# Gate broadcasts: four diagonals from VectorE and one 512-column product, in place of four 128-column products

## The chip, the cores and the metric

The kernel runs on one core of one Trainium2 chip. The metric is the device time of one execution in microseconds (us), from three timed runs of the kernel before: median 1494.13 us, 1493.53 to 1494.31 us. Lower is better. The engines are named as the profile names them: PE is TensorE (PEld its weight loads), DVE is VectorE, ACT is ScalarE, POOL is GpSimd, SP is SyncE, which issues most of the DMAs.

## The reference

The model is a two-layer trunk on 256 latent and 256 context tokens of width 1024, followed by one layer of a second model. The change touches only the modulation of the trunk. Per layer, six vectors of 1024 come from the condition; two of them, `ga1` and `ga2`, gate the two residual branches:

```python
mod = [m[:, None, :] for m in jnp.split(jax.nn.silu(c) @ w_mod[i] + b_mod[i], N_MOD, axis=-1)]
mod_c = jnp.split(jax.nn.silu(c_ctx) @ w_mod[i] + b_mod[i], N_MOD, axis=-1)
sh1, sc1, ga1, sh2, sc2, ga2 = mod
...
x = x + ga1 * rmsnorm(y, p["g_post_mix"])
xc = xc + ga1c * rmsnorm(yc, p["g_post_mix"])
...
x = x + ga2 * rmsnorm(sq_relu_mlp(hm, p["w_mlp1"], p["w_mlp2"]), p["g_post_mlp"])
```

All inputs are float32. In the last layer only the latent tokens go on, so that layer needs no context gates.

## The kernel before

**Layout.** Tokens lie on the 128 partitions in the residual stream (`X`, `Y`), so a gate, which differs by feature and not by token, must stand in the same row on all partitions: `GA` is [128, 4, 1024]; its four rows are the gates of sections 2 and 5 (`ga1`, `ga2`), each for latent and context. The modulation itself is computed by feature: `mod` has feature 128*kt + p on partition p, in one column per kt and per condition.

**Turning a gate.** One gate step makes half a gate, 512 features: column kt of `mod`, repeated over 128 columns, is the stationary operand, and the identity matrix `C_IDENT` the moving one. The product has in each row the 128 features of that column. Four such float32 products fill one bank of PSUM (L789), and ACT copies the bank to `GA` (L1316). PE waits for `mod_vec`, the semaphore of the finished column vectors.

**Where the gate steps run.** While the heads' attention runs, PE, ACT and DVE go through a list of small steps, `MOD_STEPS`, written out by hand in `fill_table`. The steps "rows" (32 weight loads against `cond`, reading two 1 MB chunks of the weight stream, L750), "features" (4 transposes, L756, then a reduction on DVE, L1991), "gate", and "cf_*" (parts of the conformer branch) all use bank 3 of PSUM. So they are a chain: PE starts step n only when ACT or DVE has read step n-1 (`mod_read`). Attention unit i has three slots for steps. In unit i PE runs scores (L945, L950), slot 0, transposes (L962), slot 1, values (L978), slot 2. DVE runs the maxima of the scores (L2139, L2140), slot 0, the probabilities (L2147, L2150), its half of the transposed probabilities (L2204), slot 1, outputs (L2210), slot 2. ACT runs slot 0, exponentials (L1522), L1585, slot 1, outputs (L1592), slot 2. Each engine runs its own list in order. In layer 0, gate steps stand in units 3, 4, 6, 7, 11, 12 (two) and 13; this text numbers them gate 1 to gate 8. Layer 1 has four: gates 9 and 10 inside the output projection (`OUT_STEPS`, L596), gates 11 and 12 at the first chunk of the MLP (`LAST_GATES`, called in `last_tile`).

**Weights.** SP loads the stream in chunks of 1 MB into four slots (L447), each when PE is through with the chunk that held the slot. ACT rounds a chunk to `w_hi` (L425), DVE subtracts to get `w_lo` (L435), and large products run in three passes of these pairs (L550, L570, L596).

**Names of DVE lines used below.** L1966 and L1967 are the statistics of the conformer's normalisation, L1981 the lower part of its last product, L1995, L1999 and L2003 finish a modulation vector. The order of all work is fixed in the program text; there is no scheduler.

Of the kernel before, what the change touches and what calls it, by code (L numbers as in the profile page):

```python
# [101 lines left out]
            MOD_STEPS += _steps  # L102
OUT_STEPS = range(len(MOD_STEPS), len(MOD_STEPS) + 3)
MOD_STEPS += [("features", DEPTH - 1, 5, 1), ("gate", DEPTH - 1, 2, 0), ("gate", DEPTH - 1, 2, 1)]
LAST_GATES = range(len(MOD_STEPS), len(MOD_STEPS) + 2)
MOD_STEPS += [("gate", DEPTH - 1, 5, half) for half in range(2)]

# [11 lines left out]
def mod_biased_count(n):  # L119

    return sum(kind == "features" and part == 1 for kind, l, sec, part in MOD_STEPS[START_STEPS:n])


def mod_vec_of(l, sec):
    return mod_vec_count(MOD_STEPS.index(("features", l, sec, 1)) + 1)
# [613 lines left out]
def pe_mod_step(k, pe, n, bank):  # L739

    kind, l, sec, part = MOD_STEPS[n]
    if n:
        pe.wait_ge(k.s("mod_read"), n)
    if kind == "rows":
        for j in range(2):
            c = At(mod_chunk(l, sec, part) + j)
            pe.wait_ge(k.w_loaded[c.slot], 16 * (c.first // SLOTS + 2))
            for kt in range(KT):
                g = kt % 4
                last = pe.matmul(k.banks(bank, 256, j * 256, slice(32 * g, 32 * g + 32)), k.cond[:, kt * 32:kt * 32 + 32],  # L750
                                 k.w[:, c.slot, kt * 256:kt * 256 + 256], start=kt < 4, stop=kt >= 4)
            last.then_inc(k.chunk_mm, 1)
    elif kind == "features":
        for kt in range(4):
            at = part * 512 + kt * 128
            last = pe.transpose(k.banks(bank, 128, kt * 128), k.rows[:, at:at + 128], k.C[:, C_IDENT:C_IDENT + 128])  # L756
        last.then_inc(k.s("mod_mm"), 1)
    elif kind == "cf_t":
        nq = 256 * CF_HALVES[l]
        k.wait(pe, "cf_conv", l, 1)  # L760
        for t in range(2):
            for kt in range(2):
                at = kt * nq + (2 * part + t) * 128
                last = pe.transpose(k.banks(bank, 128, t * 256 + kt * 128), mixer_buffers(k)["cf_acc"][:, at:at + 128],
                                    k.C[:, C_IDENT:C_IDENT + 128])
        last.then_inc(k.s("mod_mm"), 1)
    elif kind == "cf_b":
        k.wait(pe, "cf_norm", l, 1)
        for t in range(2):
            for kt in range(2):  # L770
                at = (2 * part + t) * 256 + kt * 128
                last = pe.transpose(k.banks(bank, 128, kt * 256 + t * 128), k.cft[:, at:at + 128],
                                    k.C[:, C_IDENT:C_IDENT + 128])
        last.then_inc(k.s("mod_mm"), 1)
    elif kind == "cf_pw":
        nq = 256 * CF_HALVES[l]
        k.wait(pe, "cf_act", l, CF_HALVES[l])
        for j in [part] if l == 0 else range(2):
            for kt in range(2):
                at = 1280 + kt * 256 + j * 128  # L780
                last = pe.matmul(k.banks(bank, nq, 0 if l == 0 else j * nq), k.SW[:, at:at + 128],
                                 mixer_buffers(k)["cf_acc"][:, kt * nq:kt * nq + nq], start=kt == 0, stop=kt == 1)
        last.then_inc(k.s("mod_mm"), 1)
    else:
        v, half = part // 2, part % 2
        pe.wait_ge(k.s("mod_vec"), mod_vec_of(l, sec))
        for kt in range(4):
            at = feature(l, sec) + (4 * half + kt) * 2 + v
            last = pe.matmul(k.banks(bank, 128, kt * 128), k.mod[:, at:at + 1].broadcast_to([128, 128]),  # L789
                             k.C[:, C_IDENT:C_IDENT + 128], start=True, stop=True)  # L790
        last.then_inc(k.s("mod_mm"), 1)


def start_rows(k, pe, n, j, bank):
# [488 lines left out]
def act_mod_step(k, act, n, bank):  # L1283
# [22 lines left out]
    elif kind == "cf_pw":  # L1306
        nq = 256 * CF_HALVES[l]
        act.wait_ge(k.s("mod_mm"), mod_mm_count(n + 1))
        hk = k.h_hi[:, :].rearrange("p (k n) -> p k n", k=KT)
        to = hk[:, 4 + part, :] if l == 0 else hk[:, 4:6, 0:nq]  # L1310
        src = k.banks(bank, 512) if l == 0 else k.banks(bank, 512).rearrange("p (k n) -> p k n", k=2)
        act.activation(to, src, ACT.Copy, scale=0.5).then_inc(k.s("cf_hi"), 1)
    elif kind == "gate":
        v, half = part // 2, part % 2
        act.wait_ge(k.s("mod_mm"), mod_mm_count(n + 1))
        act.activation(k.GA[:, 2 * GATE_SECTIONS.index(sec) + v, half * 512:half * 512 + 512], k.banks(bank, 512),  # L1316
                       ACT.Copy).then_inc(k.s("mod_read"), 1)


def act_start(k, act, o):  # L1320
# [632 lines left out]
    last.then_inc(k.s("cf_norm"), 1)  # L1953


def dve_mod_step(k, dve, n, bank, o=None):

    if n - 1 in [cf_statistics_at(layer) for layer in range(DEPTH)]:
        dve_cf_norm(k, dve, o, n >= FILL[1][0][0][0])
# [79 lines left out]
def dve_mixers(k, dve, o, l):  # L2039
# [206 lines left out]
        feed_lo(k, dve, out + 1, (1,))  # L2246
    dve_feed_rest(k, dve, out)
    transposed(end - 1)
    outputs(end - 1)


# [529 lines left out]
```

## Time and profile before

| what | value |
|---|---|
| timed runs | median 1494.13 us (1493.53 to 1494.31, 3 runs) |
| profiled execution | 1492.4 us, its span 1490.4 us |
| PE busy | 1434.9 us, 96% of the span |
| DVE busy | 908.4 us, 61% |
| ACT busy | 679.5 us, 46% |
| POOL busy | 37.1 us, 2% |
| granted TensorE clock, mean | 0.998 |
| the chain that ended last | PE 86%, ACT 5%, DVE 4%, DMA 3% |

The span runs from the first to the last instruction; the profiled execution's own time is 2.0 us more. "Busy" sums an engine's instructions with their modelled ends, so a busy PE may still be held back by others. In the chain of the work that ended last, each piece of time is put down to what released the next one. A row of the timeline gives start, duration, engine, line, operation, output and inputs, and in brackets how long the engine had been idle and what released it. The gate steps stand between 189.8 and 260 us (layer 0) and between 808 and 840 us (layer 1).

### The profile page before, as it was taken

What the parts mean: (1) busy time and instruction counts of PE and PEld (TensorE: products, weight loads), DVE (VectorE), ACT (ScalarE), POOL (GpSimd) and SP (SyncE); (2) the same over time, 40 slices, a digit from 0 to 9 for tenths busy, and PEclk for the clock granted to TensorE, in tenths of its full rate; (3) what the DMA queues carried; (4) which work ended last, traced back from release to release, by engine and by line L of the source; (5) the groups of instructions that cost most, each with busy time, mean ns of one, the idle gap of its engine ahead of it and who ended that gap; (6) DMA issues with size and microseconds to landing.
All of it is one profiled execution on the core that took longest, in us unless ns stands there. A gap on an engine that the chain in (4) does not pass through costs nothing.

```text
span 1490.4 us, 23388 instructions
## 1 busy us (share of the span) xinstructions
PE 1434.9 (96%) x9380; PEld 1229.4 (82%) x9380; DVE 908.4 (61%) x1394; ACT 679.5 (46%) x1084; POOL 37.1 (2%) x53
## 2 busy tenths in 40 slices
PE   5999998999999999999999999998999999999998
PEld 2787655888888888888866888997999999798996
DVE  2677455564232433468756665568998545796867
ACT  4421355553130322456145844456444564764544
POOL 0000000000000000000060000000000000000000
PEclk9999999999999999999999999999999999999999
DMA  9321575032331313236365555464445434455553
GB/s 394 144 87 71 213 296 227 1 142 85 113 97 43 142 56 141 85 113 220 123 245 237 198 187 180 147 221 170 170 170 171 146 138 142 142 197 190 178 198 114
DMA packets 33274, 235.91 MB, mean 158 GB/s; under 512 B 3680, under 2 KB 3680, under 8 KB 5408
## 3 DMA queue, kind: packets, MB, share of 16 engines
q1 hardware_dynamic: 32080, 228.31, 42.4%
q0 software_dynamic: 1104, 6.29, 1.3%
q8 instruction: 69, 1.13, 0.3%
q14 instruction: 21, 0.17, 0.0%
HBM read 233.54 MB, written 1.05 MB: 157 GB/s over the span
## 4 chain that ended last, share of the span: by engine, by line
PE 86%; ACT 5%; DVE 4%; DMA 3%; issue 1%; SPq 0%; DVEq 0%; ACTq 0%
PE ps L550 44%; PE ps L596 23%; PE ps L570 4%; DMA w<-in_stream 3%; PE ps L750 2%; PE ps L830 1%; PE ps L652 1%; PE ps L945 1%; PE ps L978 1%; ACT w_hi L425 1%; PE ps L962 1%; DMA w<-in_start 1%; PE ps L950 1%; PE ps L687 1%; PE ps L624 1%
## 5 line engine op out<-in xcount | busy, mean ns | idle before, releaser
L550 PE MATMUL ps<-h_hi,w_hi 128*128 128x256 f32 (+1 forms) x1504 | 468.6, 312 | 3.4 <-DVE h_lo L2436 0.9
L550 PE MATMUL ps<-h_hi,w_lo 128*128 128x256 f32 (+1 forms) x1504 | 464.7, 309 | 0.0
L550 PE MATMUL ps<-h_lo,w_hi 128*128 128x256 f32 (+1 forms) x1504 | 464.6, 309 | 0.0
L425 ACT ACTIVATE w_hi<-w 128x1024 fp32r<-128x1024 f32 x332 | 333.6, 1054 | 244.1 <-DMA w<-in_stream 244.0
L435 DVE TENSOR_TENSOR w_lo<-w,w_hi 128x1024 fp32r<-128x1024 f32 x332 | 391.0, 1221 | 87.7 <-ACT w_hi L425 83.3
L550 PEld LDWEIGHTS ps<-h_hi,w_hi 128*128 128x128 f32 x1504 | 287.0, 191 | 20.4 <-issue 2.9
L550 PEld LDWEIGHTS ps<-h_lo,w_hi 128*128 128x128 f32 x1504 | 287.0, 191 | 14.9 <-issue 0.5
L550 PEld LDWEIGHTS ps<-h_hi,w_lo 128*128 128x128 f32 x1504 | 286.9, 191 | 14.5
L596 PE MATMUL ps<-w_hi,g_hi 128*128 128x512 f32 x472 | 185.1, 392 | 1.8 <-DVE g_lo L2289 0.9
L596 PE MATMUL ps<-w_lo,g_hi 128*128 128x512 f32 x472 | 183.8, 389 | 0.0
L596 PE MATMUL ps<-w_hi,g_lo 128*128 128x512 f32 x472 | 183.8, 389 | 0.0
L596 PEld LDWEIGHTS ps<-w_hi,g_hi 128*128 128x128 f32 x472 | 88.6, 188 | 23.5 <-issue 3.2
L596 PEld LDWEIGHTS ps<-w_hi,g_lo 128*128 128x128 f32 x472 | 88.6, 188 | 18.7
L596 PEld LDWEIGHTS ps<-w_lo,g_hi 128*128 128x128 f32 x472 | 88.6, 188 | 17.7
L2288 DVE CAST g_hi<-R 128x1024 fp32r<-128x1024 f32 (+1 forms) x32 | 17.9, 561 | 127.0 <-ACT R L1659 127.0
L2267 DVE TENSOR_TENSOR Y<-ps,Y 128x512 f32<-128x512 f32 (+1 forms) x32 | 28.5, 889 | 99.0 <-PE ps L596 99.0
L1656 ACT ACTIVATE R<-ps 128x1024 f32<-128x1024 f32 (+1 forms) x32 | 26.0, 812 | 135.2 <-PE ps L550 126.0
L2069 DVE SCALAR_TENSOR_TENSOR U<-U,F 128x512 f32<-128x512 f32 (+1 forms) x120 | 65.0, 615 | 0.0
L570 PE MATMUL ps<-w_hi,h_hi 128*128 128x256 f32 x176 | 50.5, 287 | 0.0
L570 PE MATMUL ps<-w_lo,h_hi 128*128 128x256 f32 x176 | 49.8, 283 | 0.0
L570 PE MATMUL ps<-w_hi,h_lo 128*128 128x256 f32 x176 | 49.8, 283 | 0.0
L2463 DVE SCALAR_TENSOR_TENSOR R<-ps,F,R 128x254 f32<-128x254 f32 (+1 forms) x88 | 37.1, 477 | 14.1 <-ACT R L1797 13.4
(281 smaller groups left out, 1749.4 us busy)
## 6 DMA issues: line engine op xcount, KB each, us to landing
w<-in_stream SPq DMA_DIRECT2D x206, 1024.0 KB, 5.0
U<-in_start SPq DMA_DIRECT2D x4, 1024.0 KB, 11.7
w<-in_start SPq DMA_DIRECT2D x2, 1024.0 KB, 10.7
GA<-in_start SPq DMA_DIRECT2D x2, 1024.0 KB, 14.0
U<-in_bias POOLq DMA_DIRECT2D x2, 1024.0 KB, 6.2
SW<-in_small POOLq DMA_DIRECT2D x2, 896.0 KB, 4.9
X<-in_x SPq DMA_DIRECT2D x1, 1024.0 KB, 4.9
X<-in_ctx SPq DMA_DIRECT2D x1, 1024.0 KB, 7.1
```

Source lines behind the costliest of these rows:

```text
L425: act.activation(k.w_hi[:, c.slot, half], k.w[:, c.slot, half], ACT.Copy).then_inc(k.hi_done, 1)
L435: dve.tensor_tensor(k.w_lo[:, c.slot, half], k.w[:, c.slot, half], k.w_hi[:, c.slot, half].bitcast(f32), ALU.subtract).then_inc(k.lo_done, 1)
L550: last = pe.matmul(k.banks(2 * c.pair, n, j * (512 if tiles == 2 else n)), w[a][:, c.slot, at:at + 128], h[b][:, kt * stride:kt * stride + n],
L570: last = pe.matmul(k.banks(2 * c.pair, 256, t * (512 if n_tiles == 2 else 256)), h[a][:, at:at + 128], w[b][:, c.slot, kt * 256:kt * 256 + ...
L596: last = pe.matmul(unit_banks(k, c, tiles, t, half), h[a][:, at:at + 128], w[b][:, chunk.slot, local * 512:local * 512 + 512], start=kt == ...
L624: last = pe.matmul(unit_banks(k, c, 2, t, half), h[a][:, at:at + 128], w[b][:, chunk.slot, local * 512:local * 512 + 512], start=kt == 0 a ...
L750: last = pe.matmul(k.banks(bank, 256, j * 256, slice(32 * g, 32 * g + 32)), k.cond[:, kt * 32:kt * 32 + 32], k.w[:, c.slot, kt * 256:kt * ...
L1656: act.activation(k.R[:, j % 2, 0:2 * n].rearrange("p (t n) -> p t n", t=2), k.two(c, n), ACT.Relu).then_inc(k.act_read, 1)
L2069: ins = dve.scalar_tensor_tensor(acc[:, kt], src, w, acc[:, kt], ALU.mult, ALU.add)
L2267: dve.tensor_tensor(y, products, y, ALU.add).then_inc(k.dve_read, 1)
L2288: o.link(dve.tensor_copy(k.g_hi[:, cols:cols + 2 * n], r))
L2463: return dve.scalar_tensor_tensor(r, k.banks(2 * c.pair, 254 + tap, t * 512), k.F[:, bass.ds(tile, 1)], r, ALU.mult, ALU.add)
```

## The change

VectorE writes, into the very half row of `GA` that the gate will fill, the four 128x128 diagonal matrices that hold the gate's features: the identity, repeated four times, times the four columns, each repeated 128 times. It is one float32 operation on 128x512 elements. TensorE then multiplies once: a 128x128 matrix of ones, stationary, by these 512 columns. Each column has one element that is not zero, so the product has the gate in every row. ACT copies the bank to the same half row of `GA` as before. PE now waits for `diag`, a count of diagonals; the wait for `mod_vec` moves to VectorE. ACT's program is the same.

```diff
 OUT_STEPS = range(len(MOD_STEPS), len(MOD_STEPS) + 3)
 MOD_STEPS += [("features", DEPTH - 1, 5, 1), ("gate", DEPTH - 1, 2, 0), ("gate", DEPTH - 1, 2, 1)]
+LAST_FILLS = [FILL[DEPTH - 1][2][2][0], FILL[DEPTH - 1][3][2][0]]
 LAST_GATES = range(len(MOD_STEPS), len(MOD_STEPS) + 2)
...
+def gate_count(n):
+
+    return sum(kind == "gate" for kind, *_ in MOD_STEPS[:n + 1])
+
+
+def gate_row(k, sec, part):
+
+    v, half = part // 2, part % 2
+    return k.GA[:, 2 * GATE_SECTIONS.index(sec) + v, half * 512:half * 512 + 512]
...
     else:
-        v, half = part // 2, part % 2
-        pe.wait_ge(k.s("mod_vec"), mod_vec_of(l, sec))
-        for kt in range(4):
-            at = feature(l, sec) + (4 * half + kt) * 2 + v
-            last = pe.matmul(k.banks(bank, 128, kt * 128), k.mod[:, at:at + 1].broadcast_to([128, 128]),
-                             k.C[:, C_IDENT:C_IDENT + 128], start=True, stop=True)
-        last.then_inc(k.s("mod_mm"), 1)
+        pe.wait_ge(k.s("diag"), gate_count(n))
+        pe.matmul(k.banks(bank, 512), k.C[:, C_ONES:C_ONES + 128], gate_row(k, sec, part),
+                  start=True, stop=True).then_inc(k.s("mod_mm"), 1)
...
+def dve_diagonal(k, dve, n):
+
+    _, l, sec, part = MOD_STEPS[n]
+    v, half = part // 2, part % 2
+    at = feature(l, sec) + 8 * half
+    columns = k.mod[:, at:at + 8].rearrange("p (k v) -> p k v", v=2)[:, :, v]
+    dve.wait_ge(k.s("mod_vec"), mod_vec_of(l, sec))
+    dve.tensor_tensor(gate_row(k, sec, part).rearrange("p (k n) -> p k n", k=4),
+                      k.C[:, C_IDENT:C_IDENT + 128].unsqueeze(1).broadcast_to([128, 4, 128]),
+                      columns.unsqueeze(2).broadcast_to([128, 4, 128]), ALU.mult).then_inc(k.s("diag"), 1)
+
+
 def dve_mod_step(k, dve, n, bank, o=None):
 
+    dve_step(k, dve, n, bank, o)
+    if n + 1 < OUT_STEPS[0] and MOD_STEPS[n + 1][0] == "gate":
+        dve_diagonal(k, dve, n + 1)
+    if n in LAST_FILLS:
+        dve_diagonal(k, dve, OUT_STEPS[1 + LAST_FILLS.index(n)])
+
+
+def dve_step(k, dve, n, bank, o):
...
     dve_feed_rest(k, dve, out)
     transposed(end - 1)
+    if l == 1:
+        for n in LAST_GATES:
+            dve_diagonal(k, dve, n)
     outputs(end - 1)
```

In layer 0 a diagonal stands right behind the DVE part of the step before its gate; for gates 9 and 10 it stands behind the last step of attention units 2 and 3 of layer 1, and for gates 11 and 12 ahead of the last outputs of layer 1.

The first place is VectorE before gate 1, in unit 3 of layer 0. BN_STATS and BN_AGGR are the normalisation's statistics (`hs` is their input), the TENSOR_REDUCE behind them the maxima of the next scores. Before:

```order
L1966 BN_STATS tiny<-hs 128x6
L1967 BN_AGGR tiny<-tiny 128x2
L1966 BN_STATS tiny<-hs 128x6
L1967 BN_AGGR tiny<-tiny 128x2
L2140 TENSOR_REDUCE tiny<-ps 128x2
L2147 RECIPROCAL tiny<-tiny 128x2
```

And now:

```order
L1993 BN_STATS tiny<-hs 128x6
L1994 BN_AGGR tiny<-tiny 128x2
L1993 BN_STATS tiny<-hs 128x6
L1994 BN_AGGR tiny<-tiny 128x2
L1969 TENSOR_TENSOR GA<-C,mod 128x512
L2167 TENSOR_REDUCE tiny<-ps 128x2
L2174 RECIPROCAL tiny<-tiny 128x2
```

The diagonal (GA<-C,mod) stands between the statistics and the maxima.

The second place is TensorE at the same gate: scores (L945, L950), the gate, transposes of probabilities (L962), transposes of a features step (L756). Before:

```order
L950 MATMUL ps<-U 128x256 x2
L789 MATMUL ps<-C,mod 128x128 x4
L962 MATMUL ps<-C,U 128x128 x8
L756 MATMUL ps<-C,U 128x128 x4
L978 MATMUL ps<-U,Y 64x128 x8
```

And now:

```order
L958 MATMUL ps<-U 128x256 x2
L798 MATMUL ps<-GA,C 128x512
L970 MATMUL ps<-C,U 128x128 x8
L768 MATMUL ps<-C,U 128x128 x4
L986 MATMUL ps<-U,Y 64x128 x8
```

Nothing moves on TensorE; four instructions have become one that reads what VectorE wrote.

The third place is VectorE from gate 5 to gate 8, units 11 to 13 of layer 0 (`w_lo` is a half chunk of the output weights, `h_lo<-ps,h_hi 128x512` the end of the conformer's product). Before:

```order
L1981 SCALAR_TENSOR_TENSOR h_lo<-ps,h_hi 128x512
L2140 TENSOR_REDUCE tiny<-ps 128x2
...
L1999 SCALAR_TENSOR_TENSOR mod<-mod,F 128x16
L2140 TENSOR_REDUCE tiny<-ps 128x2
L2147 RECIPROCAL tiny<-tiny 128x2
...
L435 TENSOR_TENSOR w_lo<-w,w_hi 128x1024
L2210 TENSOR_TENSOR h_lo<-ps,h_hi 128x2x128
L435 TENSOR_TENSOR w_lo<-w,w_hi 128x1024
```

And now:

```order
L2008 SCALAR_TENSOR_TENSOR h_lo<-ps,h_hi 128x512
L1969 TENSOR_TENSOR GA<-C,mod 128x512
L2167 TENSOR_REDUCE tiny<-ps 128x2
...
L2026 SCALAR_TENSOR_TENSOR mod<-mod,F 128x16
L1969 TENSOR_TENSOR GA<-C,mod 128x512
L2167 TENSOR_REDUCE tiny<-ps 128x2
L1969 TENSOR_TENSOR GA<-C,mod 128x512
L2174 RECIPROCAL tiny<-tiny 128x2
...
L2237 TENSOR_TENSOR h_lo<-ps,h_hi 128x2x128
L1969 TENSOR_TENSOR GA<-C,mod 128x512
L447 TENSOR_TENSOR w_lo<-w,w_hi 128x1024
```

Four diagonals are added here: one ahead of the maxima of unit 11, two around those of unit 12, and one ahead of a half chunk of `w_lo` in unit 13.

## Rows read from the trace of the kernel before

**Rows 1.** Page, the chain that ended last, share of the span by engine

```profile
PE 86%; ACT 5%; DVE 4%; DMA 3%; issue 1%; SPq 0%; DVEq 0%; ACTq 0%
```

**Rows 2.** Chain in order of time, 150 to 275 us: start, duration, what

```profile
189.83 1.09 PE ps L789 x8
...
224.14 7.00 DMA w<-in_stream
...
234.75 1.93 PE ps L781 x4
```

**Rows 3.** Chain in order of time, 740 to 850 us

```profile
809.29 0.89 PE ps L789 x8
```

**Rows 4.** Timeline, gate 1: start, duration, engine, line, operation, [idle before <-releaser]

```profile
189.76 1.16 PE L789 MATMUL ps<-C,mod 128*128 128x128 f32 x8
...
190.23 0.18 DVE L1967 BATCH_NORM_AGGREGATE tiny<-tiny 128x2 f32<-128x6 f32 x1
190.33 0.66 DVE L2140 TENSOR_REDUCE tiny<-ps 128x2 f32<-128x512 f32 x1
```

**Rows 5.** DVE groups by form: shapes, count | busy us, mean ns | idle before

```profile
L2195 DVE TENSOR_TENSOR h_lo<-U,h_hi 128x512 fp32r<-128x512 f32 x1 | 0.7, 694 | 0.5 <-ACT h_hi L1576 0.5
...
L2398 DVE TENSOR_TENSOR GA<-GA,tiny 128x1024 f32<-128x1024 f32 x1 | 1.2, 1224 | 0.0
```

**Rows 6.** Timeline, gate 2

```profile
197.07 0.15 DVE L2147 RECIPROCAL tiny<-tiny 128x2 f32<-128x2 f32 x1
...
199.00 1.16 PE L789 MATMUL ps<-C,mod 128*128 128x128 f32 x8
```

**Rows 7.** Timeline, gates 3 and 4

```profile
212.19 1.16 PE L789 MATMUL ps<-C,mod 128*128 128x128 f32 x8
212.66 0.15 DVE L2147 RECIPROCAL tiny<-tiny 128x2 f32<-128x2 f32 x1
...
214.38 0.60 ACT L1316 ACTIVATE GA<-ps 128x512 f32<-128x512 f32 x1
...
215.04 0.65 PE L756 MATMUL ps<-C,U 128*128 128x128 f32 x4 [1.10 <-ACT GA L1316]
...
216.68 0.97 PEld L789 LDWEIGHTS ps<-C,mod 128*128 128x128 f32 x8 [0.76 <-DVE mod L1991]
```

**Rows 8.** Timeline, gates 5 and 6

```profile
245.07 0.69 DVE L1981 SCALAR_TENSOR_TENSOR h_lo<-ps,h_hi 128x512 fp32r<-128x512 f32 x1 [1.69 <-ACT h_hi L1312]
245.68 0.68 DVE L2140 TENSOR_REDUCE tiny<-ps 128x2 f32<-128x512 f32 x1
245.82 1.16 PE L789 MATMUL ps<-C,mod 128*128 128x128 f32 x8 [0.78 <-DVE h_lo L1981]
...
248.92 0.17 DVE L1999 SCALAR_TENSOR_TENSOR mod<-mod,F 128x16 f32<-128x16 f32 x1
...
249.91 1.16 PE L789 MATMUL ps<-C,mod 128*128 128x128 f32 x8
```

**Rows 9.** Timeline, gates 7 and 8

```profile
253.87 1.23 DVE L435 TENSOR_TENSOR w_lo<-w,w_hi 128x1024 fp32r<-128x1024 f32 x1 [1.90 <-ACT w_hi L425]
...
255.01 0.42 DVE L2210 TENSOR_TENSOR h_lo<-ps,h_hi 128x256 fp32r<-128x256 f32 x1
...
255.57 1.23 DVE L435 TENSOR_TENSOR w_lo<-w,w_hi 128x1024 fp32r<-128x1024 f32 x1
...
258.78 0.66 PE L962 MATMUL ps<-C,U 128*128 128x128 f32 x4 [1.47 <-ACT U L1585]
```

**Rows 10.** Timeline of layer 1, where the diagonals of gates 9 to 12 fall

```profile
780.43 0.70 DVE L2139 TENSOR_TENSOR ps<-ps,U 128x512 f32<-128x512 f32 x1
...
784.86 1.07 PE L750 MATMUL ps<-w,cond 128*32 128x256 f32 x16 [0.58 <-DMA w<-in_stream]
...
788.64 0.70 DVE L2139 TENSOR_TENSOR ps<-ps,U 128x512 f32<-128x512 f32 x1 [0.88 <-PE ps L945]
...
819.49 0.42 DVE L2210 TENSOR_TENSOR h_lo<-ps,h_hi 128x256 fp32r<-128x256 f32 x1 [4.26 <-ACT h_hi L1592]
```

More of the change, by code:

```diff
@@ L1313, in act_mod_step @@
     elif kind == "gate":
-        v, half = part // 2, part % 2
         act.wait_ge(k.s("mod_mm"), mod_mm_count(n + 1))
-        act.activation(k.GA[:, 2 * GATE_SECTIONS.index(sec) + v, half * 512:half * 512 + 512], k.banks(bank, 512),
-                       ACT.Copy).then_inc(k.s("mod_read"), 1)
+        act.activation(gate_row(k, sec, part), k.banks(bank, 512), ACT.Copy).then_inc(k.s("mod_read"), 1)
 def act_start(k, act, o):
```

## The prediction, written before the change was run

> **What bounds the kernel now.** I read the chain that ended last first: 86% of the span is TensorE's own work and only some 12% belongs to other engines and DMAs [rows 1]. So a change that removes TensorE time gains it nearly everywhere, and one that makes TensorE wait loses it. Then I read the same chain in order of time around the gate steps. In layer 0 the gates lie in a stretch where PE, ACT and DVE hand one PSUM bank back and forth; TensorE's queue goes from group to group with no slack: the chain at gate 1 is the four products themselves, 1.09 us [rows 2]. In layer 1 they lie inside dense products of the weight stream and cost 0.89 us each [rows 3]. Last I read the timeline at each of the twelve gates, to see for each what DVE was doing when TensorE started its products, since the new operation stands in DVE's fixed order and TensorE must now wait for it.
>
> **TensorE's part: nearly nothing.** Removed are 12 x 4 products of 128 columns (8 records a gate, two passes a product), added 12 x 1 of 512 columns. The same number of float32 columns streams through in both cases. The trace has products of exactly the new form, 128x128 weights by 512 columns in float32, at line 781: two of them took 1.93 us on the chain, so one takes 0.97 us [rows 2]. The four old ones take 1.09 us there and 0.89 us in the dense stretch [rows 2, 3]. So a gate lies between a gain of 0.12 (1.09 to 0.97) and a loss of 0.08 (0.89 to 0.97). What the six removed weight loads are worth is seen in the same rows: 0.97 / 8 = 0.12 us for 128 columns in a wide product, 0.11 to 0.14 in a narrow one. The loads are hidden either way. I take a gain of 0.03 a gate, near the middle of the two, on the seven gates at which TensorE is what the next work waits for (1, 5, 6 and the four of layer 1): -0.2 us. The range of this term is 7 x -0.12 = -0.8 to +0.3 (the loss on the four dense ones).
>
> The Trainium skill ("TensorE: Matmul & The Clock Gate", section "Back-to-back issue gap") says that in a stream of load and product pairs the spacing is set by both, and gives about 81 ns for a 128-column product, against about 56 ns for one by itself. By that rule, as an estimate from that page, six pairs less would save about 6 x 25 ns = 0.15 us a gate and 1.8 us over the twelve, and the sum below would come down to about +0.4. The rows of this kernel show no such gap, since its float32 passes stream long enough to cover a load.
>
> **VectorE's part.** Added are 12 operations on 128x512 float32 elements with two SBUF inputs. The same operation with plain inputs takes 0.694 us, and one with a column repeated along the row, as here, takes 1.224 us for 1024 columns, no more than a plain one of that size (1.23 us) [rows 5, 9]. So the diagonal takes 0.69 us. L1981, of the same size and duration, began at 245.07; DVE's next operation began 0.61 later and TensorE, which waited for it, at 245.82, 0.06 after its end [rows 8]. So a diagonal delays what follows on DVE by 0.61, and TensorE can start 0.75 after it began. Bounds: 0.66, as the reduction over as many elements [rows 4], to 0.70 [rows 10]. No row repeats both inputs; were that read at half rate, the nearest row is the one of 1024 columns, 1.22 [rows 5], and the four places that cost below would cost 2.1 more. Nothing points to it, and I give it less than 2 in 100.
>
> What this does, gate by gate. Behind each diagonal wait the maxima or probabilities on DVE, for these ACT's exponentials, and for these TensorE's transposes two units later.
>
> *Gate 1.* TensorE started at 189.76. The last statistics began on DVE at 190.23 and the maxima at 190.33 [rows 4]. The diagonal takes the place of the maxima: 190.35 to 191.04, and TensorE starts at 191.10. It stalls 1.34 us, and ACT's copy, its exponentials and the next transposes all follow TensorE. It waits because the diagonal was put behind the statistics, not because its input is late. This is the largest term: +1.34.
>
> *Gate 2.* The diagonal starts at 197.07, where the reciprocal stood, and ends at 197.76; TensorE comes at 199.00 [rows 6]. Cost 0: the cover is 1.2 us. With gate 1's delay all of this moves together.
>
> *Gates 3 and 4.* Diagonal 3 starts at 212.66 and ends at 213.35; TensorE would have started at 212.19 and starts at 213.41, 1.22 late [rows 7]. But ACT is at its exponentials and reads the bank only at 214.38; the wide product, done 0.97 to 1.16 us after its start, is ready at 214.4 to 214.6. So only 0 to 0.2, I take 0.09, passes on to L756 at 215.04. Diagonal 4 comes behind a reduction that released TensorE at 216.68 [rows 7]; it fits beside the scores (0.76 us idle) with 0 to 0.1 left over; I take 0.03. Both: +0.12. If ACT's cover were gone, gate 3 alone would cost 1.2.
>
> *Gate 5.* TensorE waited for L1981 and started at 245.82; the maxima began at 245.68 [rows 8]. The diagonal is 245.68 to 246.37, TensorE starts at 246.43: +0.61.
>
> *Gate 6.* The diagonal starts 0.2 after L1999, at 249.13, and is through at 249.82 + 0.06 = 249.88; TensorE came at 249.91 [rows 8]. Cost 0, with a cover of only 0.03.
>
> *Gates 7 and 8.* Diagonal 7 pushes back probabilities, but DVE then has 1.90 us idle before it can do `w_lo` at 253.87 [rows 9]: 0. Diagonal 8 starts 0.34 after L2210 (255.35: like L1981 it lets the next begin 0.08 before its own end) and delays the next half of `w_lo` from 255.57 to 255.96. Behind it stand the last maxima, the exponentials, and TensorE at 258.78, which waits for ACT [rows 9]: +0.38.
>
> *Gates 9 to 12.* Diagonal 9 delays the maxima that start at 780.43 by 0.6, and the probabilities behind them; TensorE in this stretch waits for chunks of the stream (784.86), which were asked for before that [rows 10]: 0. Diagonal 10 stands in an idle time of 0.88 before 788.64, 0.27 more than it needs: 0. Diagonals 11 and 12 (1.3 us together) fall into 4.26 us of idle before 819.49: 0 [rows 10].
>
> **The sum.** 1.34 + 0.12 + 0.61 + 0.38 = 2.45 us of waiting, less 0.2 on TensorE: +2.2 us. Nothing downstream gives it back: where TensorE waits for a DMA in layer 0, the chunk was asked for when TensorE had read the one before it (224.14, 7.00 us [rows 2]), so the wait moves along. The profiled execution took 1492.4 us (span 1490.4, 2.0 around it): the sum gives 1494.6 for it. It lies 1.7 below the median of the timed runs, 1494.13, to which the forecast belongs: 1496.3 us, +0.15%. I call a difference within 0.2% (3.0 us) no change, since a measurement of this kernel can't tell less.
>
> **The rivals.**
>
> *B, slower: the wide product is dearer for TensorE than its old four.* Place: the four gates in dense streams, where the old group costs 0.89. If there the load of the weights behind a wide product lies open, it costs 0.97 plus one load of 0.12 (0.97 / 8 [rows 7]), 0.20 more, and 0.8 over the four; the other three gain nothing. Then +2.45 + 0.8 = +3.3: 1497.4. It decides from 0.14 us a dense gate on. For it: at 0.97, no row shows a wide float32 product inside the dense passes. Against it: consecutive passes of line 781 are 0.48 apart, with loads inside them.
>
> *C: the stalls before 224 us are given back at the DMA.* If the stream, not its request, sets when the chunk of 224.14 lands (7.00 us for 1 MB [rows 2]), then 1.4 of the 2.45 vanish: +0.8, 1494.9. Against it: the transfer starts with the request, directly behind TensorE's last read.
>
> *D: the six loads less are worth something after all.* The largest gain the rows allow, 0.12 on seven gates, gives 2.45 - 0.8 = +1.6; with the full 1.16 of the modelled group against 0.97 it is 0.19 on seven, 1.3, and +1.1: 1495.2. The skill's rule on spacing, above, would bring it to +0.4. For it: 1.09 on the chain; against it: 0.89 in the dense stretch.
>
> *E, faster than before:* nothing in the rows pays for it; TensorE's largest gain (1.3) is less than the stall at gate 1 alone. It would need gate 1's product not to be late.
>
> **How the numbers follow.** A, the sum: 0.50. B: 0.25. C: 0.10. D: 0.12. E: 0.03. The forecast is A's, 1496.3. A's own spread is about 1 us, so 0.08 of it lies above 1497.1, the bound of no change. Slower: 0.25 + 0.08 = 0.33, and 0.02 for C and D missing with a longer diagonal, 0.35; faster 0.03; no change the rest, 0.62. The range takes in C and D from below and most of B from above: 1494.3 to 1498.2.
>
> **What would show it.** In the profile after, TensorE must sit idle about 0.8 to 1.3 us before gate 1's product with the diagonal as releaser, and about 1.4 (0.78 + 0.61) before gate 5's; gates 2, 6 and 9 to 12 must not wait for a diagonal. The diagonal must take 0.69 us. The product's group on the chain must be 0.9 to 1.0. The same landmarks must be late by about 1.3 us at the end of unit 3, 1.45 at 224 us, and 2.4 at 260 us, and keep that to the end. The prediction is wrong if the lag at 260 us is small, or if it is there and gone at 750 us.

## The result: 4.5 to 5.8 us slower, the stalls as worked out, two terms missing

The changed kernel took 1498.96 us (median of 13 runs, 1496.26 to 1502.18), the kernel before 1494.43 beside it (13 runs, 1493.27 to 1498.41): ratio 1.0029, 95% interval 1.0020 to 1.0039. The forecast was 1496.3, its range ended at 1498.2, and "no change" was held likeliest; by the prediction's own bound of 0.2% (3.0 us) what came is "slower". Repeated on two other chips the changed kernel gave 1499.67 against 1494.13 (ratio 1.0036, 1.0023 to 1.0050) and 1499.93 against 1494.09 (1.0041, 1.0029 to 1.0053).

The profiled execution of the changed kernel took 1496.26 (span 1494.3), 3.9 over that of before. Its share by engine on the chain that ended last [rows 1]:

```profile
PE 86%; DVE 5%; ACT 4%; DMA 4%; issue 1%; SPq 0%; DVEq 0%; ACTq 0%
```

The chain in order of time, 150 to 275 us (start, duration, what), answers to [rows 2]. In the new line numbers a gate's product is L798, a diagonal L1969:

```profile
190.79 0.59 DVE GA L1969
191.38 0.14 issue
191.52 1.10 PE ps L798 x2
...
214.43 0.61 DVE GA L1969
...
215.18 1.11 PE ps L798 x2
...
226.06 7.66 DMA w<-in_stream
...
248.33 0.61 DVE GA L1969
...
249.08 1.10 PE ps L798 x2
...
258.58 0.60 DVE GA L1969
```

Four diagonals stand on the chain, at gates 1, 3, 5 and 8, which are the places the prediction named. At gate 1 [rows 4] the timeline reads (start, duration, engine, line, idle before it and who ended that):

```profile
190.71 0.66 DVE L1969 TENSOR_TENSOR GA<-C,mod 128x512 f32<-128x512 f32 x1
191.29 0.69 DVE L2167 TENSOR_REDUCE tiny<-ps 128x2 f32<-128x512 f32 x1
191.52 1.10 PE L798 MATMUL ps<-GA,C 128*128 128x512 f32 x2 [1.30 <-DVE GA L1969]
```

At gates 5 and 8 [rows 8, 9]:

```profile
249.08 1.10 PE L798 MATMUL ps<-GA,C 128*128 128x512 f32 x2 [1.47 <-DVE GA L1969]
```

```profile
262.30 0.66 PE L970 MATMUL ps<-C,U 128*128 128x128 f32 x4 [1.85 <-ACT U L1591]
```

The waits were 0.78 and 1.47 us before [rows 8, 9]; both are longer, by 0.69 and 0.38. All twelve diagonals (view of line L1969: duration min/median/max in ns):

```profile
L1969 DVE TENSOR_TENSOR GA<-C,mod x12: 659/681/689, 190.7 to 818.6; 128x512 f32<-128x512 f32 x12
```

In the dense stretch the wide product took this place on the chain (740 to 850 us) [rows 3]:

```profile
785.93 7.93 DMA w<-in_stream
...
812.17 0.86 PE ps L798 x2
```

The lag of a place is how much later the same piece of TensorE's work starts in the trace after than in the one before. It gives the account of this one pair of traces:

| place | lag | added there | forecast |
|---|---|---|---|
| 180 us, before any gate | +0.34 | +0.34 | 0 |
| behind gate 1 | +1.69 | 1.31 | 1.34 |
| behind gates 3, 4 | +1.91 | 0.23 | 0.12 |
| chunk of 226 us landed | +2.57 | 0.66 | 0 |
| behind gate 5 | +3.17 | 0.61 | 0.61 |
| behind gate 8 | +3.51 | 0.35 | 0.38 |
| 850 us | +2.78 | -0.7 | -0.1 for gates 9 to 12 |
| 1018 us | +2.78 | 0 | 0 |
| 1040 us | +3.92 | 1.1 | 0 |
| end | +3.87 | 0 | 0 |

The stalls at the gates add up to 2.5 us (forecast 2.45). Four things are not gates. The +0.34 at 180 us is the rest of two: the first contraction starts 0.75 earlier (28 us), and a stretch at half clock there lasts twice as long as before (until 33 in place of 31 us), 1.1 more. Then come +0.66 where TensorE waits for a chunk, -0.6 around another such wait at 783 us (that chunk took 7.93 us after, 8.52 before), and +1.1 at 1026 to 1033 us. The last shows in the windows of 2 us (length; busy time and count of PE, PEld, DVE, ACT and POOL; then the granted clock; then DMA share and GB/s). After:

```profile
1024.00:1026.00 2.00, 1.05 (x7) 0.84 (x8) 1.90 (x6) 1.52 (x5) 0.00 (x0) 1.00 0.75 213
1026.00:1028.00 2.00, 1.21 (x6) 0.94 (x7) 1.97 (x4) 1.66 (x4) 0.00 (x0) 0.56 0.77 324
1028.00:1030.00 2.00, 2.00 (x9) 2.00 (x10) 1.71 (x5) 1.62 (x4) 0.00 (x0) 0.50 0.00 0
```

Before, at the same work:

```profile
1022.00:1024.00 2.00, 1.04 (x9) 0.84 (x7) 1.93 (x5) 1.97 (x7) 0.00 (x0) 1.00 0.78 307
1024.00:1026.00 2.00, 0.83 (x8) 0.66 (x7) 1.87 (x5) 1.63 (x4) 0.00 (x0) 1.00 0.40 168
1026.00:1028.00 2.00, 1.91 (x18) 1.71 (x16) 1.81 (x3) 1.22 (x3) 0.00 (x0) 1.00 0.04 8
```

The granted clock was at its half level (0.50, which is 1.2 of 2.4 GHz) behind a stretch in which TensorE had been busy little over half the time (1.05 and 1.21 of 2 us). Before, it had been busy no more than that at the same work (1.04 and 0.83), and the clock stayed full. So the half level came in the one execution and not in the other. No gate lies there.

### The profile page after: what moved, and what is told of

It reads as the page before. It is cut to its first block, busy times and chain, and to the rows that moved or that the text cites. A ratio compares the mean times of both kernels' runs of the same rounds, so it can differ in the third digit from the quotient of the medians.

```text
span 1494.3 us, 23256 instructions
## 1 busy us (share of the span) xinstructions
PE 1435.8 (96%) x9308; PEld 1224.3 (82%) x9308; DVE 914.8 (61%) x1406; ACT 679.0 (45%) x1084; POOL 36.9 (2%) x53
## 3 DMA queue, kind: packets, MB, share of 16 engines
q8 instruction: 69, 1.13, 0.3%
HBM read 233.54 MB, written 1.05 MB: 157 GB/s over the span
## 4 chain that ended last, share of the span: by engine, by line
PE 86%; DVE 5%; ACT 4%; DMA 4%; issue 1%; SPq 0%; DVEq 0%; ACTq 0%
PE ps L562 43%; PE ps L608 23%; PE ps L582 4%; DMA w<-in_stream 3%; PE ps L762 2%; PE ps L838 1%; PE ps L664 1%; PE ps L953 1%; DMA U<-in_start 1%; PE ps L986 1%; PE ps L699 1%; PE ps L970 1%; ACT w_hi L437 1%; DVE w_lo L447 1%; PE ps L958 1%
```

## The experiments

The questions: does the 0.66 at the chunk belong to the change, and the clock too? Fifteen runs followed: twelve other kernels, the changed one twice more and the one before once more. "Before" is the kernel before, timed on the same chip beside them; times without a word are medians in us. Each execution has its mean granted clock. Within the kernels, over all executions, the time goes down by 0.88 us for each 0.001 of mean clock more (+-0.05; a +- here is one standard error). "At equal clock" is a difference of means corrected by that. The edits are shown shortened: slices of the constants, start and stop flags and tables are left out.

**The kernel before, unaltered.**

> The kernel before once more, to have the granted clock and the span of several executions of it. The profile after shows the stalls of the sum (2.5 us by 262 us), but also one stretch at half clock, 1026 to 1033 us, that the profile before does not have, worth 1.3 us. Theory 1 (the changed kernel meets such stretches more often): mean granted clock of nearly all executions 0.998, times within 1 us of 1494.4, while the changed kernel had 0.993 to 0.997. Theory 2 (such stretches come by chance to both): clocks spread over 0.993 to 0.998 here too, and times over 4 us or more.

1494.96 us, before 1495.36 (35 runs, 1492.51 to 1501.21), ratio 0.9990 (0.9978 to 1.0003). Its profile has a span of 1495.8, 5.4 longer than the first one, with half-clock stretches at 30, 1028 and 1296 us where the first has only the one at 28 us. (In the last 10 us, behind TensorE's last product, the clock is low in every trace; those are left out throughout.) So the kernel by itself spreads over 9 us, and the three runs from which the forecast started (1493.53 to 1494.31) showed none of it. Over all the experiments before has 129 executions, median 1494.67, mean clock 0.9957.

**Waits kept, old products.**

```
-        pe.matmul(banks(bank, 512), C_ONES, gate_row(k, sec, part))
+        for kt in range(4):
+            pe.matmul(banks(bank, 128, kt * 128), k.mod[:, at:at + 1].broadcast_to([128, 128]), C_IDENT)
```

> The changed kernel with its diagonals and TensorE's wait for them, but the four old 128-column products in place of the wide one. Theory A (all of the loss is waiting, the wide product is worth 0.03 us a gate): 0.2 to 0.4 us slower than the changed kernel, 1499.2. Rival B (the wide product is dearer than the old four): 0.8 us or more faster than the changed kernel, 1498.2 or less. The stalls before gates 1, 3 and 5 stay in either case: lag against before of 1.3 us at 200 us, 2.4 to 2.5 at 262 us but for the transfer near 226 us.

1499.85 (12 runs), ratio 1.0025 (1.0013 to 1.0037): 4.5 over before, at equal clock +3.1 +-0.4. The diagonals and the waits for them make most of the loss without the wide product. The changed kernel wasn't timed on this chip, so the 0.2 to 0.4 us between the two can't be judged. The trace shows the same stalls (gates 1, 5 and 8), the chunk in 7.20 us, and this behind gate 1:

```profile
190.00:192.00 2.00, 0.71 (x7) 0.64 (x6) 1.93 (x7) 0.00 (x0) 0.00 (x0) 1.00 0.92 373
192.00:194.00 2.00, 2.00 (x12) 2.00 (x11) 0.57 (x2) 1.14 (x4) 0.00 (x0) 0.52 0.88 373
194.00:196.00 2.00, 2.00 (x19) 1.67 (x19) 1.06 (x3) 1.78 (x4) 0.00 (x0) 0.63 0.03 12
```

TensorE idles for the diagonal (1.29 us), and runs at half clock behind it. That cost another 1.5 us: the lag against before is +1.63 at the gate and +3.18 at 196 us. The same came behind gate 8.

**Wide product, no waits** (the product reads 512 columns of constants, so the gates' values are left out; there are no diagonals).

> The wide product alone: no diagonals, no wait for them; TensorE multiplies the ones by 512 constant columns instead (so the gates are wrong: this part of the computation is left out). Theory A: -0.2 us against before, 1494.2, clock as before. Rival B: +0.8 us, 1495.2. If the lower clock comes from the wide product and not from the waiting, the granted clock is 0.993 to 0.997 here and the time 1495 or more.

1496.42 (12 runs), ratio 1.0005 (0.9992 to 1.0018); at equal clock +0.7 +-0.4. The mean clock, 0.9952, is that of before beside it (0.9951), so the wide product doesn't lower it. In the trace gate 1 takes 0.04 us off the lag (+0.82 to +0.78; the prediction's term was 0.03) and the lag is +0.77 ahead of the chunk, but the chunk took 7.66 us, not 7.00. The 0.66 us is there without a single stall.

**Diagonals written early** (into idle times of VectorE, gates 1 and 3 to 8):

```
-    if n + 1 < OUT_STEPS[0] and MOD_STEPS[n + 1][0] == "gate":
-        dve_diagonal(k, dve, n + 1)
+    for part in EARLY.get(MOD_STEPS[n], ()):
+        dve_diagonal(k, dve, MOD_STEPS.index(part))
```

> The changed kernel with the diagonals of layer 0 in places where VectorE is idle for longer than they take: that of gate 1 two steps earlier, those of gates 3 and 4 behind a features step of unit 5, those of gates 5 to 8 behind a features step of unit 9. Theory A (the loss is the diagonals' places on VectorE): no TensorE wait for a diagonal at any gate, lag against before at 262 us within 0.3 us, time 1494.2. If diagonals cost wherever they stand (through the bank chain or the ports): 1496 or more.

1497.23 (12 runs), ratio 1.0009 (0.9997 to 1.0020), 2.6 us under the kernel with the waits on the same chip. No stall at any gate: from 175 us to the wait for the chunk its lag goes from +0.26 to +0.22. Then the chunk, 7.75 us, and +0.97. The time is not the 1494.2 expected but lies where the expectation's rival put it (1496 or more). Part of that is the chip, where before had 1495.36, not 1494.4; at equal clock +1.0 +-0.4 is left over before, of which the late chunk is 0.75. (For the same reason its lag is +0.91 at 262 us, not within 0.3.) The rival's reason, that diagonals cost wherever they stand, finds nothing in the trace.

**The changed kernel again.**

> The changed kernel again, unaltered. Theory 1 (the added stalls are 2.5 us, and what lies beyond that is the clock's and the start's variation from execution to execution): median 1.5 to 4 us above before, the profile shows TensorE idle 1.3 us at gate 1 again, and half-clock stretches at other places than in the first profile of this kernel, or none. Theory 2 (each new stall also brings a half-clock stretch behind it, so that the change costs more than its stalls): median 4 us or more above before, and half-clock stretches behind gate 1 (190 us in) or behind gates 5 and 8 (246 to 264 us in).

1499.67 (5 runs), before 1494.13 (21 runs): 5.5 over, in theory 2's range. The stalls are the same to 0.01 us: 1.30, 0.23, 0.60, 0.36. The chunk took 7.74 us, and this time half clock came behind gate 8:

```profile
260.00:262.00 2.00, 0.92 (x2) 0.09 (x1) 1.97 (x5) 0.57 (x3) 0.00 (x0) 1.00 0.00 0
262.00:264.00 2.00, 1.22 (x13) 0.88 (x13) 0.75 (x3) 2.00 (x5) 0.00 (x0) 1.00 0.03 8
264.00:266.00 2.00, 2.00 (x8) 1.59 (x7) 1.79 (x2) 2.00 (x5) 0.00 (x0) 0.62 0.00 0
266.00:268.00 2.00, 2.00 (x7) 1.55 (x6) 1.97 (x7) 2.00 (x3) 0.00 (x0) 0.53 0.00 0
```

It cost 1.6 us (lag against before +4.00 at 263 us, +5.57 at 268).

**Diagonals of gates 1 to 5 written twice.**

```
+        spare = gate_row(k, 2, part + 1) if (sec, part) in ((2, 0), (2, 1), (2, 2)) else gate_row(k, 5, 3)
+        dve.tensor_tensor(spare, C_IDENT, columns, ALU.mult)
         dve.tensor_tensor(gate_row(k, sec, part), C_IDENT, columns, ALU.mult)
```

> The diagonals of gates 1 to 5 written twice, the first time into a row that is not read. Theory 1: TensorE idles 0.7 us longer at gates 1 and 5 (2.0 and 1.3 us), a little at gates 2 to 4, so 1.4 to 2.2 us over the changed kernel, about 4.5 us over before. Rival (the wait for a diagonal is not what costs, the time is from elsewhere): no more than 0.3 us over the changed kernel. Theory 2: over 3 us above the changed kernel, with a half-clock stretch behind gate 1.

1503.47 (5 runs), before 1494.13: ratio 1.0060 (1.0046 to 1.0074), 3.8 over the changed kernel. That is more than theory 1's 1.4 to 2.2 and in theory 2's range. The chain shows two diagonals at each place, and the product behind those of gate 1 is longer (1.79 in place of 1.10 us), at half clock:

```profile
191.28 0.58 DVE GA L1971
191.85 0.61 DVE GA L1974
192.60 1.79 PE ps L798 x2
```

Half clock followed gate 1 (192 to 196 us) and gate 5 (254 to 258 us). In this trace the stalls grew by 2.0 us and the half clock cost 3.2. But over the five runs the mean clock, 0.9944, is no lower than the changed kernel's on the same chip (0.9942), and at equal clock the difference is still 3.7 (+-0.6). So that longer stalls cost is shown; that the 1.7 us beyond them are clock, as theory 2 has it, is not.

**Only gate 1's diagonal early.**

> Only gate 1's diagonal moved ahead, to the step that ends the features' first half; all others stay where the change puts them. Theory 1: gate 1's stall of 1.3 us goes, the others (1.2 us) stay: 1.2 to 1.4 us under the changed kernel, 1.2 us over before. Theory 2: more than that, 2 us or more under the changed kernel.

1496.92 (11 runs), before 1494.13: ratio 1.0012 (1.0003 to 1.0021), 2.8 us under the changed kernel on the same chip, and 1.4 (+-0.5) under it at equal clock. Gate 1 has no stall (lag +1.92 at 189, +1.89 at 192 us), gates 3, 5 and 8 keep theirs (0.23, 0.60, 0.35). The stall was worth its 1.3 us; what is beyond that goes with the clock (mean 0.9956 against 0.9942).

**TensorE kept busy at 25 us, in the kernel before.**

```
+    for _ in range(4):
+        pe.matmul(banks(2 * first.pair, 512), C_ONES, k.C[:, 0:512], start=True, stop=True)
     contraction_half(k, pe, first, h, 0, (0, 1), ready)
```

> The kernel before, with four products of a matrix of ones by 512 constants put in front of the first contraction, into the bank that this overwrites: TensorE is busy there where it had been idle for 3.5 us (25 to 28 us in). Theory 1 (the kernel's own variation comes from half-clock stretches behind TensorE's idle times): the half-clock stretch of 28 to 32 us in is gone or under 2 us long, and the time is 0.5 to 1.5 us under before. Rival (the stretch at 28 us isn't caused by the idle time ahead of it): the granted clock falls there all the same, and the time is that of before or 1 us above it.

1493.77 (11 runs), before 1494.13 (ratio 0.9998, 0.9989 to 1.0007). The time can't be told from before's, so the 0.5 to 1.5 us expected were not seen, but the clock can: mean 0.9974 against 0.9957. Before had 0.50 at 28 to 30 and 0.67 at 30 to 32 us; with the fillers:

```profile
26.00:28.00 2.00, 2.00 (x6) 0.76 (x4) 0.88 (x3) 1.87 (x4) 0.00 (x0) 1.00 1.04 438
28.00:30.00 2.00, 1.89 (x6) 0.97 (x6) 1.84 (x5) 1.59 (x5) 0.00 (x0) 1.00 1.00 418
30.00:32.00 2.00, 1.73 (x19) 0.71 (x18) 1.68 (x3) 0.52 (x2) 0.00 (x0) 1.00 1.02 426
```

**What makes the chunk late.** By now six traces with the wide product had a chunk of 7.66 to 7.75 us, and four with the old products one of 7.00 to 7.22. The view of DMA queues shows one more difference. There is a queue "instruction" that moved 69 packets, 1.13 MB, in the execution, 16 KB each, which this text takes for fetches of instructions, and one of these falls near this chunk. After, 230.5 to 231.5 us, 4.8 us behind the chunk's issue (packets, MB, share of 16 engines):

```profile
q8 instruction: 1, 0.02, 6.0%
```

Before, 223.5 to 224.5 us, 0.2 us ahead of the issue:

```profile
q8 instruction: 1, 0.02, 7.7%
```

6.0% of 1 us on 16 engines is 0.96 us of one engine (an estimate from this row). Fetches lie some 180 to 340 records of TensorE (products and loads) apart in this part of the two traces (once 114); each wide product takes 12 out of its stream. So the next kernels give TensorE's stream instructions back, in its idle time at 25 us.

**Early diagonals, four wide fillers (16 instructions).**

> The kernel with the diagonals moved ahead (no stall at a gate), and four products of ones by 512 constants in front of the first contraction, which are 16 instructions of TensorE. Theory F (the chunk that TensorE waits for at about 225 us lands 0.6 us later in every kernel with the wide product because a block of TensorE's instructions is fetched about 4.8 us behind its issue, which the 12 instructions fewer a gate have moved there): with 16 of 48 instructions given back the fetch is still 2.5 to 4.5 us behind the issue, and the chunk takes 7.6 to 7.8 us. Rival (the transfer's own variation, or the wide product itself): 7.0 to 7.8 us, whatever the fetch does. The half-clock stretch at 28 us is gone in both cases, and the time is 0.8 to 1.5 us under that of the kernel with early diagonals.

1493.52 (11 runs), before 1494.54 (ratio 0.9995, 0.9986 to 1.0004). The fetch moved further than expected, to 0.12 us ahead of the issue, and the chunk took 6.76 us where 7.6 to 7.8 were expected. My guess of where the fetch falls was wrong: counting instructions doesn't give it. (In the kernel before, the same sixteen left it where it was, 0.2 us ahead.) The link between a fetch behind the issue and a late landing held.

**Early diagonals, twelve narrow fillers (48 instructions).**

> The same, but with twelve products of 128 columns in front of the first contraction in place of the four of 512: 48 instructions of TensorE, as many as the change takes out of gates 1 to 4, with the same TensorE time of some 3.5 us. Theory F: the fetch is back where it is in the kernel before, within 0.5 us of the issue, and the chunk takes 7.0 to 7.25 us from issue to landing; the time is 0.5 us under the kernel with four fillers. Rival (the wide product or other work of the changed kernel is what makes the chunk late): 7.6 to 7.8 us.

1493.25 (11 runs; ratio 0.9992, 0.9983 to 1.0001). Fetch 1.15 us ahead of the issue, chunk 6.42 us, less than before's 7.00 and than the 7.0 to 7.25 expected. The times of this kernel and the last can't be told apart.

```profile
223.83 6.42 DMA w<-in_stream
```

**The changed kernel with the four fillers.**

> The changed kernel, diagonals and waits where the change puts them, with four products of ones by 512 constants in front of the first contraction (16 instructions of TensorE ahead of gate 1). If the late chunk at 226 us comes from the fetch of TensorE's instructions: the fetch falls within 0.3 us of the chunk's issue, the chunk takes 6.7 to 7.1 us in place of 7.66 and 7.74, the stalls at the gates stay as they are (1.30, 0.23, 0.60, 0.35 us), and with the half-clock stretch at 28 us gone as well the time is 1.5 to 2.5 us under the changed kernel. Rival (chunk late because of the wide product or the late diagonals): 7.6 us or more, whatever the fetch does.

1497.25 (11 runs), before 1494.09 (ratio 1.0014, 1.0004 to 1.0024), 2.7 under the changed kernel on the same chip. Stalls 1.31, 0.23, 0.60, 0.36; fetch 0.25 us ahead of the issue; chunk 6.70 us. This is the changed kernel with sixteen instructions of TensorE added, all 200 us ahead of the chunk, and the late chunk is gone. The other engines' programs are the same, so it is TensorE's stream whose fetches move. The fillers also keep TensorE busy at 25 us: the mean clock is 0.9968 against 0.9940, and at equal clock the kernel is 1.1 (+-0.9) under the changed one, where the chunk gained 0.8 to 1.0.

**TensorE kept busy while it waits for the diagonals.**

```
+        for _ in range({1: 4, 5: 2, 8: 1}.get(gate_count(n), 0)):
+            pe.matmul(banks(bank, 128), C_ONES, C_IDENT, start=True, stop=True)
         pe.wait_ge(k.s("diag"), gate_count(n))
```

> The changed kernel, with four, two and one products of 128 columns in front of the waits of gates 1, 5 and 8, into the bank that the gate overwrites: TensorE is busy while it waits for the diagonals, and each gate begins as late as in the changed kernel or up to 0.3 us later. If half-clock stretches follow the new idle times: none between 186 and 270 us, mean clock 0.9955, the time 0.5 to 1 us under the changed kernel from this. The 16 instructions at gate 1 should also bring the fetch back to the issue of the chunk, which then takes about 7.0 us, another 0.7 us. Rival (the lower clock of the changed kernel is chance): clock and time as the changed kernel's, but for the chunk's 0.7 us.

1499.95 (5 runs), before 1494.09. No half clock between 186 and 270 us, mean clock 0.9960 against 0.9940 in the changed kernel beside it, and the chunk in 7.15 us with the fetch 0.14 ahead of its issue. But the time is the changed kernel's, and at equal clock 1.3 (+-0.8) over it. In the trace it lost 1.0 us against before at a chunk at 484 us and 1.5 at the chunk at 787 us. Whether its fillers did that isn't known. That the clock stays up when TensorE is busy in these waits was seen, the gain in time was not.

**The changed kernel a third time.**

> The changed kernel unaltered, on the same chip as the two. Stalls of 1.30, 0.23, 0.60 and 0.35 us at gates 1, 3, 5 and 8, the fetch 4.8 us behind the chunk's issue and the chunk 7.7 us long; the median 4 to 5 us over before; half-clock stretches behind gate 1, 5 or 8 in this profile with a chance of a half.

1499.93 (6 runs), 5.8 over before where 4 to 5 were expected. Stalls 1.31, 0.22, 0.61, 0.36; fetch 4.64 us behind the issue, chunk 7.49; half clock at 28 and 1028 us, none behind a gate.

**Fillers at three places, in the kernel before** (25 us, and between the pieces of the first chunks):

```
+PADS = {("mix2", 0, 0): 2, ("mix2", 0, 2): 3, ("mix2", 0, 4): 4, ("mix2", 1, 0): 4, ("ffn", 0, 4): 7, ("ffn", 1, 0): 4}
...
+        for _ in range(PADS.get((name, t, kt), 0)):
+            pe.matmul(spare half of the bank, C_ONES, C_IDENT, start=True, stop=True)
         if kt % 2 == 0:
             pe.wait_ge(k.s("h", name), ...)
```

> The kernel before with TensorE's idle times filled at three places: four products of 512 columns at 25 us, and 13 and 11 of 128 columns between the pieces of the first chunks behind the normalisations at about 1020 and 1290 us. Theory 1 (half-clock stretches follow TensorE's idle times, and make most of the kernel's variation): none of the three stretches is left or they are rarer, the mean granted clock is 0.997 or more, and the time is 1 to 2.5 us under before. Rival (the fillers cost what they save): within 0.5 us of before, with the products behind the fillers later by as much.

1492.46 (11 runs), before 1494.54 (ratio 0.9990, 0.9981 to 0.9999), mean clock 0.9986 against 0.9961. Yet its own profile (span 1494.7) shows half clock at 30 us in spite of the fillers, and again at 794 us: they make it rarer, not impossible.

**Everything together**: wide product, early diagonals, twelve narrow fillers, later fillers.

> Everything that the runs so far point to in one kernel: the wide product, the diagonals of gates 1 and 3 to 8 written ahead of need, twelve products of 128 columns in the idle time ahead of the first contraction (which also move the fetch of TensorE's instructions off the transfer that lands at about 231 us), and the fillers between the pieces of the first chunks at about 1020 and 1290 us. Expected 2.5 to 3.5 us under before, from 1 to 1.7 us for the kernel with the pads alone and 1 us for the later fillers; the chunk at 224 us takes 6.3 to 6.6 us; mean clock 0.998 or more. If the gains don't add (rival: the fillers at 1020 and 1290 us cost what they save): 1 to 2 us under before, as with the pads alone.

1492.25 (12 runs, 1490.43 to 1494.09), before 1493.94: ratio 0.9985 (0.9976 to 0.9993), mean clock 0.9990, the chunk in 6.45 us. It is under both kernels: before by 1.7 us, and the changed kernel (24 executions in all, median 1499.4) by some 7. The gains did not fully add (1.7 where 2.5 to 3.5 were expected). And nothing shows that the wide product has a part in them: the kernel before with fillers at three places and its old products was 2.1 under before on another chip, and at equal clock this one is 0.5 +-0.3 over before. Its gain goes with the clock, which was full at both places where others fell:

```profile
28.00:30.00 2.00, 1.17 (x9) 0.97 (x8) 1.54 (x4) 1.63 (x4) 0.00 (x0) 1.00 1.00 406
1028.00:1030.00 2.00, 1.64 (x14) 1.45 (x14) 1.56 (x6) 2.00 (x7) 0.00 (x0) 1.00 0.00 0
```

The chunk of about 225 us, by where the fetch falls (us from the chunk's issue, to about 0.05; less than 0 is ahead of it):

| kernel | fetch | issue to landing, us |
|---|---|---|
| twelve narrow fillers; all together | -1.15; -1.14 | 6.42; 6.45 |
| changed + four fillers; early + four | -0.25; -0.12 | 6.70; 6.76 |
| before; again; filler at 25; at three places | -0.2 (all) | 7.00; 7.22; 7.04; 7.06 |
| fillers at the gates; waits with old products | -0.14; +0.29 | 7.15; 7.20 |
| changed, three times | +4.78; +4.84; +4.64 | 7.66; 7.74; 7.49 |
| wide only; early; gate 1 early; written twice | +4.8 (all) | 7.66; 7.75; 7.75; 7.69 |

A fetch 4.6 us or more behind the issue went with 7.49 us or more in each of seven traces, and one at -0.25 to +0.3 with less in each of eight. Among these eight the chunk still took from 6.70 to 7.22 us, so something else moves it too, by up to 0.5 us. The wide product by itself isn't the cause: it stands in both groups.

## Why the prediction was wrong

*The bound and the places: right.* TensorE is on the chain with 86%, four diagonals came onto it, at the four gates named; the others did not.

*The stalls: right.* 1.31, 0.23, 0.61 and 0.35 measured in three executions within 0.02, where 1.34, 0.12, 0.61 and 0.38 were forecast; only the wait passed on at gate 3 was twice its term. The diagonal took 0.68 us, forecast 0.69, and the case of a half-rate operand did not occur. From the diagonal's end to TensorE it was 0.14 us, not 0.06. Moving gate 1's diagonal alone gave back its 1.3, moving seven gave back all.

*TensorE's part: right for what it counted.* 0.03 a gate, in the dense stretch too (0.86 against 0.89). Rival B needed 1.09 there and falls; D, which needed a gain of 0.12 a gate or more, falls with it. The Trainium skill's rule on spacing ("TensorE: Matmul & The Clock Gate", section "Back-to-back issue gap") would have saved 0.15 us a gate, by the estimate in the prediction; the traces show a fifth of that for these float32 products.

*C: wrong.* The chunk was issued 1.92 us later (226.06 for 224.14), the lag that the stalls had made by then, and its wait grew instead of shrinking. The 0.6 us given back at 783 us are the transfer's own spread: 7.93 us after and 8.52 before, but 7.93 in the unchanged kernel's second trace too, and 8.50 and 8.04 in the changed one's others.

*The step that failed is the sentence "Nothing downstream gives it back: ... so the wait moves along"*, with its duration of 7.00 us held fixed. It left out that twelve instructions fewer a gate move the fetches of TensorE's own instructions. One fetch went from 0.2 us ahead of the chunk's issue to 4.8 behind, into the transfer, and the chunk took 7.49 to 7.75 us in all seven executions, of five kernels, where it did: 0.5 to 0.75 more than the first trace of before (7.00), 0.3 to 0.5 more than its second (7.22). That the fetch delays it is shown as far as landings went with the place of the fetch, in the changed kernel too when only TensorE's stream was moved (7.66 to 6.70). That it does so by holding one of the 16 DMA engines for about 1 us is argued, not shown.

*And the time was taken from stalls alone:* the clock is in no term of the sum. In the traces the idle time at a gate was followed by half clock in three of the seven executions of kernels with late diagonals and no fillers at the gates (behind gate 8; behind 1 and 8; behind 1 and 5), never in the ten others between 150 and 300 us. Each time cost 1.5 to 1.7 us. The mean clock says the same: 0.9944 over the 24 runs of the changed kernel, 0.9957 over 129 of before, 0.0013 or 1.1 us. On their chips, the kernels that have gate 1's stall and no fillers were 0.0011 to 0.0018 under before, those without the stall and without fillers 0.0004 or less. But of the changed kernel's own three traces only one has half clock behind a gate; all three have 3 to 7 us of it at about 28 us, as before's two traces have (3 us each), and all three have 6 to 7 us at about 1028 us, where before's two have none and 3 us and no gate lies. How much of the 1.1 us the stalls cause, and by what way, stays open.

The sum as it should have been: 2.5 of stalls, -0.2, 0.66 for the chunk, 1.1 for the clock: 4.1, against 4.5 measured first and 5.5 and 5.8 on the other chips. The start was also too low: 1494.13 from three runs, where 129 give 1494.67. *The range* was too narrow for the same reason: it knew the sizes of the steps and not the spread of the executions, whose standard deviation is 1.8 us for the changed kernel's 13 runs. What stays open is the rest, 0.4 to 1.7 us: at equal clock the changed kernel was 3.7 +-0.5 and 4.1 +-0.8 over before on the other chips, where stalls and chunk make 3.0.

## What to carry to other kernels

Work added on a second engine costs the first engine's wait, and can cost the clock behind that wait as well; so write an operand one step ahead of its use, in an idle time of its engine, and not directly before it. A trace of one execution shows what a step costs, not how the executions spread: ask for runs of the unchanged kernel before a forecast of a change of 0.1%. Taking instructions out of a stream, or adding some, moves its fetches, and a chunk that an engine waits for can land later for it: 6.42 us from issue with the fetch well ahead, up to 7.75 with it inside the transfer.

## What was not expected of the hardware

A 16 KB fetch of TensorE's instructions inside a 1 MB transfer came with 7.5 to 7.75 us from issue to landing, one 1.15 us ahead of the issue with 6.4. TensorE's clock fell to its half level for 3 to 10 us (10 at 1028 us in the trace with gate 1's diagonal early), behind idle times as short as 1.3 us (gate 1), in some executions and not in others at the same place. Products into a bank about to be overwritten, put into the idle times, brought the mean clock from 0.996 to 0.999; in the kernel before that gave 2.1 us of the median and 1.3 of the mean.
